# Sums of squares of single tiles: from one f32 matmul to two rounded passes, and what is reordered around them

## The chip, the core and the metric

One core of a Trainium2 chip runs the whole kernel. The metric is device time in microseconds (us); lower is better. Of the engines, TensorE (PE, its weight loads PEld), VectorE (DVE), ScalarE (ACT) and the DMA queue of SyncE (SP) work here. Each takes its instructions in the order of the program and waits on semaphores that the others raise.

## What is computed

Two encoder layers over 272 tokens (16 learned ones and 256 of the input) of width 2048. Each layer normalises its input, projects it with one matrix into the columns of four branches, and adds the projected branch outputs back:

```python
h = rms_norm(x, norm_w)
proj = jnp.einsum('bld,dn->bln', h, w_in)
(aq, ak, av, ag, bq, bk, bv, bg, cq, ckv, ckr, cg, du, dg) = jnp.split(proj, split_points, axis=-1)
ya = diff_attention(aq, ak, av, ...)      # 4 heads, rms_norm of q, k and of the head's output
yb = axial_gqa(bq, bk, bv, ...)           # 4 query heads, 2 key heads, rms_norm of q and k
yc = latent_attention(cq, ckv, ckr, ...)  # q and kv are projected up from normed latents
yd = multiscale_pool(du, ...)
y = jnp.concatenate([ya * silu(ag), yb * silu(bg), yc * silu(cg), yd * silu(dg)], axis=-1)
return x + jnp.einsum('bln,nd->bld', y, w_out)

def rms_norm(x, w):
    return x * lax.rsqrt(jnp.mean(x * x, axis=-1, keepdims=True) + EPS) * w
```

Every such norm of a query, a key or a head's output needs the sum of squares over 64 or 128 rows of a tile. It is these sums that the change is about. Layer 1 computes queries for 256 tokens only.

## The kernel before

Activations stand transposed: channels on the 128 partitions, the 272 tokens along the free axis. Weights stream from HBM into `raw` in chunks of 128 x 1024. A chunk is split into two rounded halves: ACT copies it to `w_hi` (form fp32r), DVE subtracts and writes `w_lo`. The activations are split the same way (`h_hi`/`h_lo`, `y_hi`/`y_lo`), and a product is three rounded passes (`three`, lines 725 to 727). There are four buffers of split weights (`RING`); the split of chunk s + 3 is queued in slot s, and it waits until chunk s - 1 is done.

A **slot** is the time of one chunk; there are 129 a layer. A projection of 256 columns is a **pair** of two tiles and takes four slots. The order of everything else is set by three tables, `AT_TENSOR`, `AT_SCALAR` and `AT_VECTOR`: `make_plan` gives each stage a slot, the table of an engine adds a fraction, and the engine takes its stages in the order of the sums. `MOVED` shifts single stages.

The stages that the change touches:

- `lift` (ACT) copies a finished tile out of one of two banks (`dense`); `rescale` (DVE) multiplies it with the token's norm.
- `rope_pre` (ACT) squares a tile into `sq` and, for tiles that are rotated, writes a weighted copy `qw`; `rope_stat` (PE) sums the squares over the rows with a matrix of ones in plain f32 into `norm_ps`; `rope_fin` makes the inverse root on ACT (lines 1114 and 1115, into the one buffer `rn`) and finishes the tile on DVE (five instructions, lines 1389 to 1398). Tiles aq, ak, qr and kr stand alone (11 a layer). Tiles bq, bk, qn and kn come in pairs, whose squares DVE adds first (`sq_sum`).
- `sub_pre`, `sub_stat`, `sub_fin` do the same for the output of each of the four A heads, which lies in `o_ps`. The first DVE instruction of `sub_fin` (line 1421) reads `o_ps` and signals `o_taken`. The next head's first `pv` (PE, line 924) writes that bank and waits for it. `sub_slot` puts the stage off where a slot is taken by a tile of its kind.
- `score`, `s_max`, `s_exp`, `s_scale`, `p_turn`, `p_out`, `pv` are the steps of one block of queries: PE, DVE, ACT, DVE, PE, ACT, PE.
- Slots 16 to 20 are the up-projection of branch C. Its 13 tiles go through the same two banks, so that a tile waits until `up_out` (ACT) has copied the one before the last. `up_out` copies all tiles of a chunk in one stage.
- Slots 21 to 28 do the gates of branch C (`gate`) and the norms of kr, qn, kn and qr.

Of the kernel before, what the change touches and what calls it, by code (L numbers as in the profile page):

```python
# [110 lines left out]
def score_steps(layer):  # L111
# [13 lines left out]
AT_SCALAR = dict(rope_fin=-0.166, lat_fin=0.07, mix_out=0.09, lat_pre=0.097, sub_fin=0.1, rope_pre=0.11,  # L125
                 y_split=0.66, xscale=0.283, sub_pre=0.439, x_out=0.55, p_out=0.56, gate=0.65, s_exp=0.579,
                 lift=0.6, up_out=0.705, split=0.71, x_square=0.72, y_gate=0.73, y_lat=0.72, lam_exp=0.793, v_out=1.297)
AT_VECTOR = dict(sq_sum=0.2, rope_mid=0.25, s_max=-0.418, lam_dot=-0.35, sub_fin=-0.345, rope_fin=-0.34, lat_fin=0.055, head_out=0.17,
# [4 lines left out]
MOVED = {**{("lift", l, 3, 0): -0.55 for l in range(DEPTH)},  # L133
# [4 lines left out]
def make_plan(at_engine):  # L138
# [17 lines left out]
    for l in range(DEPTH):  # L156
# [49 lines left out]
        at(s + 8, ("rope_pre", l, "kr", 0, None))  # L206
        at(s + 9, ("rope_stat", l, "kr", 0))
        at(s + 10, ("rope_fin", l, "kr", 0))

        for c in range(U_CHUNKS):  # L210
            at(s + 4 + c, ("up_out", l, c))
        posts = [("qn", 0), ("kn", 0), ("qr", 0), ("qr", 1), ("qn", 1), ("kn", 1)]
        for n, (key, i) in enumerate(posts):
            s = g0 + pair_slot(4) + 1 + n + (2 if i else 0)
            at(s, ("rope_pre", l, key, i, None))
            if key in PAIRED:
                at(s, ("sq_sum", "rope", l, key, i))
# [39 lines left out]
def build(nc, xt, w_stream, params, lam_rows, consts, out):  # L257
# [31 lines left out]
    sq = sb("sq", [128, 4, L])  # L289
    qw = sb("qw", [128, 2, L])  # L290
# [27 lines left out]
    ident, ones, halves = const("ident", 128), const("ones", 128), const("halves", 128)  # L318

# [59 lines left out]
    lam_ready, lam_exp = sem("lam_ready"), sem("lam_exp")  # L379
    tails_zero = sem("tails_zero")  # L380
# [100 lines left out]
    for stg in vector_plan:  # L481
# [7 lines left out]
        if stg[0] == "sq_sum":  # L489
# [226 lines left out]
    def _(pe):  # L716
# [102 lines left out]

        def norm_free(*stage):  # L820
# [17 lines left out]
        def rope_stat(l, key, i):  # L838
            t0 = rope_from(l, key)
            if key in PAIRED:  # L840
                pe.wait_ge(summed, sum_no[("rope", l, key, i)])
            else:
                pe.wait_ge(pre_done, pre_no[("rope_pre", l, key, i)])
            norm_free("rope_stat", l, key, i)
            sums = nc.tensor.matmul(norm_ps[:, t0:L], halves, sq[:, 2 * parity("rope_stat", l, key, i), t0:L],  # L845
                                    start=True, stop=True)
# [62 lines left out]
        def pv(l, n):  # L909
# [4 lines left out]
            if branch == "c":  # L914
                pe.wait_ge(up_taken, UP_TILES * (l + 1))
# [27 lines left out]
    def _(act):  # L943
# [98 lines left out]
        def up_out(l, c):  # L1042
            for j in range(up_tiles(c)):
                ps = wait_tile(act, l, "up", c, j)
                q0 = first_query(l)
                if c < 2:
                    i, out_ = 2 * c + j, q_st[:, 2 * c + j, q0:L]
                    free = (scores_ready, store_free(l, "c", "q", i))
                elif c == 2:
                    out_, free = c_st[:, 6 + j, q0:L], (scores_ready, store_free(l, "c", "q", j))  # L1050
                elif c == 3:
                    out_, free = k_st[:, j, :], (scores_ready, store_free(l, "c", "k", j))
                else:
                    n = K_BLOCKS[j][1]
                    out_, free = v_st[0:n, j, :], (pv_done, sums_before[store_free(l, "c", "v", 3)])
                if free[1]:
                    act.wait_ge(*free)
                src = ps[0:K_BLOCKS[j][1], :] if c == 4 else ps[:, 0:L - q0] if c < 3 else ps[:, 0:L]
                signal(nc.scalar.activation(out_, src, ACT.Copy), up_taken, UP_TILES * l + up_no(c, j))  # L1059

# [8 lines left out]
        def rope_pre(l, key, i, j):  # L1069
# [31 lines left out]
        def sub_pre(l, n):  # L1101
# [3 lines left out]
            signal(nc.scalar.activation(sq[:, 2 * parity("sub_stat", l, n), t0:L], o_ps[:, t0:L], ACT.Square), pre_done,  # L1105
# [68 lines left out]
        def s_exp(l, n):  # L1174
# [6 lines left out]
            for m in (0, 1):  # L1181
                signal(nc.scalar.activation(probs[0:nq, k % 2, m, :], s_ps[m][0:nq, 0:L], ACT.Exp,  # L1182
                                            bias=stat[0:nq, 2 + m:3 + m], scale=SCALE[b],
                                            accum_out=stat[0:nq, 4 + m:5 + m]), exp_done, 2 * k + m + 1)

        def p_out(l, n):
# [7 lines left out]
            for m in range(1 if b == "a" else 2):  # L1194
# [4 lines left out]
                if m == 0 and b != "a":  # L1199
# [5 lines left out]
                   up_out=up_out, rope_pre=rope_pre,  # L1205
# [9 lines left out]
    def _(dve):  # L1215
# [49 lines left out]
        def lam_dot(_):  # L1265
# [6 lines left out]
            signal(nc.vector.memset(stat[:, :], 0.0), lam_ready, 1)  # L1272

        def lam_out(_):
            dve.wait_ge(lam_exp, 1)
            for l in range(DEPTH):
# [5 lines left out]
                link(nc.vector.tensor_scalar(sub_w[:, c], pcol(l, "sub"), 1.0 - li, None, ALU.mult))  # L1282
# [47 lines left out]
        def sq_sum(what, l, key, i=None):  # L1330
# [14 lines left out]
            signal(nc.vector.tensor_tensor(a, a, b, ALU.add), summed, n)  # L1345

# [70 lines left out]
        def sub_fin(l, n):  # L1417
# [3 lines left out]
            signal(nc.vector.scalar_tensor_tensor(ta[:, t0:L], o_ps[:, t0:L], sub_w[:, l:l + 1], rn[:, t0:L],  # L1421
# [47 lines left out]
        def s_max(l, n):  # L1469
# [187 lines left out]
```

## Time and profile before

| | before |
|---|---|
| median of 3 runs | 913.04 us (912.84 to 913.1) |
| the profiled execution, its own time | 912.77 us |
| its span, first to last instruction | 911.0 us |
| granted TensorE clock | 1.00 (the level of 2.4 GHz) throughout |
| busy: PE / DVE / ACT | 99% / 70% / 64% of the span |

The profiled execution lies 0.27 us under the median of the runs. PE's busy time is modelled: matmuls overlap, so the time that counts is from the start of one to the start of the next. In the timeline an idle stretch stands behind an instruction in brackets, with what ended it; in the tables of stretches each engine's busy time stands with its number of instructions.

### The profile page before, as it was taken

What the parts mean: (1) busy time and instruction counts of PE and PEld (TensorE: products, weight loads), DVE (VectorE), ACT (ScalarE), POOL (GpSimd) and SP (SyncE); (2) the same over time, 40 slices, a digit from 0 to 9 for tenths busy, and PEclk for the clock granted to TensorE, in tenths of its full rate; (3) what the DMA queues carried; (4) which work ended last, traced back from release to release, by engine and by line L of the source; (5) the groups of instructions that cost most, each with busy time, mean ns of one, the idle gap of its engine ahead of it and who ended that gap; (6) DMA issues with size and microseconds to landing.
All of it is one profiled execution on the core that took longest, in us unless ns stands there. A gap on an engine that the chain in (4) does not pass through costs nothing.

```text
span 911.0 us, 18111 instructions
## 1 busy us (share of the span) xinstructions
PE 899.7 (99%) x7054; PEld 858.4 (94%) x7054; DVE 637.0 (70%) x1071; ACT 585.5 (64%) x1045; POOL 0.2 (0%) x4
## 2 busy tenths in 40 slices
PE   8999999999999999999999999999999999999998
PEld 7998998999999999999999989999999999999998
DVE  7785887768777776766665658876687667666552
ACT  7678756678666667745554588566686666675331
POOL 0000000000000000000000000000000000000000
PEclk9999999999999999999999999999999999999999
DMA  8654343343444343445455544334425344445562
GB/s 332 260 188 142 134 142 132 109 139 129 140 141 142 138 148 128 145 149 192 166 195 185 186 155 169 119 119 161 158 93 186 128 151 145 149 171 185 187 201 78
DMA packets 22997, 143.83 MB, mean 158 GB/s; under 512 B 2560, under 2 KB 4736, under 8 KB 6528
## 3 DMA queue, kind: packets, MB, share of 16 engines
q1 hardware_dynamic: 22768, 142.64, 44.0%
q8 instruction: 56, 0.92, 0.4%
q14 instruction: 29, 0.24, 0.1%
q10 hardware_dynamic: 144, 0.04, 0.0%
HBM read 140.57 MB, written 2.10 MB: 157 GB/s over the span
## 4 chain that ended last, share of the span: by engine, by line
PE 89%; ACT 7%; DVE 2%; issue 1%; DMA 1%; SPq 0%; ACTq 0%; DVEq 0%
PE dense L725 25%; PE dense L727 24%; PE dense L726 24%; PE s_ps L889 4%; PE o_ps L924 4%; ACT w_hi L1014 2%; PE norm_ps L845 2%; PE t_ps L905 2%; DVE w_lo L1319 1%; ACT qw L1087 1%; DMA x<-xt_dram 1%; PE swap_ps L860 0%; ACT sq L1084 0%; PE norm_ps L727 0%; PE swap_ps L727 0%
## 5 line engine op out<-in xcount | busy, mean ns | idle before, releaser
L725 PE MATMUL dense<-h_hi,w_hi 128*128 128x272 f32 (+2 forms) x1440 | 427.1, 297 | 1.5 <-DVE h_lo L1299 0.9
L727 PE MATMUL dense<-h_hi,w_lo 128*128 128x272 f32 (+2 forms) x1440 | 412.6, 287 | 0.0
L726 PE MATMUL dense<-h_lo,w_hi 128*128 128x272 f32 (+2 forms) x1440 | 410.6, 285 | 0.0
L1319 DVE TENSOR_TENSOR w_lo<-raw,w_hi 128x1024 fp32r<-128x1024 f32 (+1 forms) x257 | 313.3, 1219 | 88.4 <-ACT w_hi L1014 82.3
L1014 ACT ACTIVATE w_hi<-raw 128x1024 fp32r<-128x1024 f32 (+1 forms) x257 | 271.3, 1056 | 68.7 <-PE dense L727 53.9
L725 PEld LDWEIGHTS dense<-h_hi,w_hi 128*128 128x128 f32 x1440 | 271.3, 188 | 8.2 <-issue 3.8
L726 PEld LDWEIGHTS dense<-h_lo,w_hi 128*128 128x128 f32 x1440 | 271.5, 189 | 1.3
L727 PEld LDWEIGHTS dense<-h_hi,w_lo 128*128 128x128 f32 x1440 | 271.1, 188 | 0.0
L725 PE MATMUL dense<-y_hi,w_hi 128*128 128x272 f32 (+1 forms) x500 | 143.1, 286 | 2.3 <-ACT q_st L1059 1.3
L727 PE MATMUL dense<-y_hi,w_lo 128*128 128x272 f32 (+1 forms) x500 | 142.7, 285 | 0.0
L726 PE MATMUL dense<-y_lo,w_hi 128*128 128x272 f32 (+1 forms) x500 | 142.4, 285 | 0.0
L725 PEld LDWEIGHTS dense<-y_hi,w_hi 128*128 128x128 f32 x500 | 94.3, 189 | 3.5 <-issue 1.9
L727 PEld LDWEIGHTS dense<-y_hi,w_lo 128*128 128x128 f32 x500 | 94.4, 189 | 0.0
L726 PEld LDWEIGHTS dense<-y_lo,w_hi 128*128 128x128 f32 x500 | 94.0, 188 | 0.0
L1039 ACT ACTIVATE row<-dense 128x272 f32<-128x272 f32 (+2 forms) x80 | 31.4, 393 | 68.7 <-PE dense L727 67.8
L1475 DVE TENSOR_REDUCE stat<-s_ps 128x1 f32<-128x272 f32 (+1 forms) x80 | 35.1, 439 | 35.6 <-PE s_ps L889 33.6
L1327 DVE TENSOR_TENSOR row<-row,rinv 128x272 f32<-128x272 f32 (+2 forms) x80 | 34.9, 437 | 29.6 <-ACT row L1039 27.5
L1114 ACT ACTIVATE rn<-norm_ps,eps_c 128x272 f32<-128x272 f32 (+1 forms) x50 | 24.2, 484 | 35.6 <-PE norm_ps L845 24.1
L1182 ACT ACTIVATE probs<-s_ps,stat 128x272 f32<-128x272 f32 (+1 forms) x80 | 38.9, 486 | 11.5 <-DVE stat L1476 9.0
L1308 DVE TENSOR_TENSOR x<-x,dense 128x272 f32<-128x272 f32 (+1 forms) x28 | 12.0, 429 | 46.7 <-PE dense L727 46.7
L924 PE MATMUL o_ps<-p_t,v_st 128*128 128x128 f32 (+1 forms) x288 | 38.6, 279 | 1.1 <-ACT p_t L1198 1.1
L924 PEld LDWEIGHTS o_ps<-p_t,v_st 128*128 128x128 f32 x288 | 35.9, 191 | 2.7 <-ACT p_t L1198 2.2
(161 smaller groups left out, 813.4 us busy)
## 6 DMA issues: line engine op xcount, KB each, us to landing
raw<-w_stream_dram SPq DMA_DIRECT2D x128, 1024.0 KB, 4.8
out_dram<-x SPq DMA_DIRECT2D x8, 256.0 KB, 6.3
x<-xt_dram SPq DMA_DIRECT2D x3, 544.0 KB, 8.9
raw<-w_stream_dram SPq DMA_DIRECT2D x3, 512.0 KB, 7.5
con<-consts_dram SPq DMA_DIRECT2D x1, 984.0 KB, 7.4
x<-xt_dram SPq DMA_DIRECT2D x2, 272.0 KB, 4.8
raw<-w_stream_dram SPq DMA_DIRECT2D x2, 256.0 KB, 4.6
d_w<-consts_dram SPq DMA_DIRECT2D x2, 256.0 KB, 5.1
```

What stands on the lines that cost most here:

```text
L725: nc.tensor.matmul(ps, whi, xhi, start=first, stop=False)
L726: nc.tensor.matmul(ps, whi, xlo, start=False, stop=False)
L727: return nc.tensor.matmul(ps, wlo, xhi, start=False, stop=last)
L889: mm = nc.tensor.matmul(s_ps[m][0:nq, 0:L], queries[half, q:q + nq], keys[half, :], start=n_part == 0, stop=n_part == len(parts) - 1)
L924: mm = nc.tensor.matmul(o_ps[:, c:c + nq], v_st[:, b, 128 * vh:128 * vh + 128], p_t[:, m, b, 0:nq], start=b == 0, stop=b == 2)
L1014: signal(nc.scalar.activation(w_hi[:, g % RING, 0:n], raw[:, e % RAW, CHUNK * half:CHUNK * half + n], ACT.Copy), hi_ready, g + 1)
L1039: signal(nc.scalar.activation(tile_place(l, p, j), ps[:, 0:L - tile_from(l, kind, j)], ACT.Copy), lifted, scaled_no[(l, p, j)])
L1114: link(nc.scalar.activation(rn[:, t0:L], norm_ps[:, t0:L], ACT.Ln, scale=1.0 / width, bias=eps_c[:, 0:1]))
L1182: signal(nc.scalar.activation(probs[0:nq, k % 2, m, :], s_ps[m][0:nq, 0:L], ACT.Exp, bias=stat[0:nq, 2 + m:3 + m], scale=SCALE[b], accum_o ...
L1319: signal(nc.vector.tensor_tensor(w_lo[:, g % RING, 0:n], raw[:, e % RAW, CHUNK * half:CHUNK * half + n], w_hi[:, g % RING, 0:n].bitcast(F3 ...
L1327: signal(nc.vector.tensor_tensor(out_, out_, rinv[:, tile_from(l, PAIRS[p][0], j):L], ALU.mult), scaled, scaled_no[(l, p, j)])
L1475: link(nc.vector.reduce_max(stat[0:nq, m:m + 1], s_ps[m][0:nq, 0:L], AX.X))
```

## The change

- The 15 single sums of squares a layer (aq, ak, kr, qr and the A heads) are no longer one f32 matmul but two rounded passes (`two`), with the rounded squares `sq_hi` and the rest `sq_lo`. ACT writes `sq_hi` with one more copy in `rope_pre` and `sub_pre`; DVE writes `sq_lo` in a new stage `sq_low`, and PE waits for that (`summed`). The matrices of ones are copied to the rounded form once.
- Those `rope_stat`, `sub_stat`, `rope_fin` and `sub_fin` stages come one slot later.
- `rope_pre` moves from 0.11 to 0.62 of its slot, behind the lifts and the steps of the blocks of queries. `sq_sum` of the paired tiles moves from 0.2 to 0.64.
- `up_out` copies one tile a stage. In the first three chunks the second tile's copy stands behind the split of the weights. The split for chunk 18 is queued a slot earlier.
- Small buffers are merged: `lam_sum`, `neg_lam`, `sub_w`, `eps_c` and `one_c` move into other tensors.

```diff
+UP_TILES = (2, 2, 2, 4, 3)
-AT_SCALAR = dict(... rope_pre=0.11,
-                 ... up_out=0.705, split=0.71, ... y_lat=0.72, ...)
-AT_VECTOR = dict(sq_sum=0.2, ...
+AT_SCALAR = dict(... rope_pre=0.62,
+                 ... up_out=0.705, up_next=0.715, split=0.71, ... y_lat=0.74, ...)
+AT_VECTOR = dict(sq_sum=0.64, sq_low=0.64, lat_sum=0.2, ...
-MOVED = {**{("lift", l, 3, 0): -0.55 for l in range(DEPTH)},
+MOVED = {**{("lift", l, 3, 0): -0.55 for l in range(DEPTH)}, **{("split", l, 18): -0.98 for l in range(DEPTH)},
...
                     at(s, ("rope_pre", l, kind, i0 + j, j))
-                    at(s, ("rope_stat", l, kind, i0 + j))
-                    at(s + 1, ("rope_fin", l, kind, i0 + j))
+                    at(s, ("sq_low", "rope", l, kind, i0 + j))
+                    at(s + 1, ("rope_stat", l, kind, i0 + j))
+                    at(s + 2, ("rope_fin", l, kind, i0 + j))
...
         for c in range(U_CHUNKS):
-            at(s + 4 + c, ("up_out", l, c))
+            for j in range(UP_TILES[c]):
+                at(s + 4 + c, ("up_next" if c < 3 and j else "up_out", l, c, j))
...
                 at(s, ("sub_pre", l, n))
-                at(s, ("sub_stat", l, n))
-                at(s + 1, ("sub_fin", l, n))
-                at(s + 1, ("y_split", "sub_fin", l, n))
+                at(s, ("sq_low", "sub", l, n))
+                at(s + 1, ("sub_stat", l, n))
+                at(s + 2, ("sub_fin", l, n))
+                at(s + 2, ("y_split", "sub_fin", l, n))
...
+        def two(ps, table, hi, lo):
+
+            nc.tensor.matmul(ps, table, hi, start=True, stop=False)
+            return nc.tensor.matmul(ps, table, lo, start=False, stop=True)
...
-            square = nc.scalar.activation(sq[:, 2 * half, t0:L], src, ACT.Square)
-            if branch:
-                link(square)
-                square = nc.scalar.activation(qw[:, half, t0:L], src, ACT.Copy, scale=pcol(l, key))
-            signal(square, pre_done, pre_no[("rope_pre", l, key, i)])
+            link(nc.scalar.activation(sq[:, 2 * half, t0:L], src, ACT.Square))
+            link(nc.scalar.activation(qw[:, half, t0:L], src, ACT.Copy, scale=pcol(l, key)))
+            signal(nc.scalar.activation(sq_hi[:, half, t0:L], sq[:, 2 * half, t0:L], ACT.Copy),
+                   pre_done, pre_no[("rope_pre", l, key, i)])
...
+        def sq_low(what, *of):
...
+            signal(nc.vector.tensor_tensor(sq_lo[:, half, t0:L], sq[:, 2 * half, t0:L],
+                                           sq_hi[:, half, t0:L].bitcast(F32), ALU.subtract), summed,
+                   sum_no[(what, *of)])
```

What the tables do to the order is seen at three places, all in layer 0. The first is ACT in the up-projection, from the copy of its first tile on (line 1059 before, 1075 after); `dense0` and `dense1` are the two banks, `w_hi` are splits, `y_hi<-c_st` is the split of the latent ckv. Before:

```order
L1059 ACTIVATE q_st<-dense0 128x272
L1059 ACTIVATE q_st<-dense1 128x272
L1014 ACTIVATE w_hi<-raw 128x1024
L1143 ACTIVATE y_hi<-c_st 128x544
L1059 ACTIVATE q_st<-dense0 128x272
L1059 ACTIVATE q_st<-dense1 128x272
L1014 ACTIVATE w_hi<-raw 128x1024
```

and after the change:

```order
L1075 ACTIVATE q_st<-dense0 128x272
L1030 ACTIVATE w_hi<-raw 128x1024
L1075 ACTIVATE q_st<-dense1 128x272
L1160 ACTIVATE y_hi<-c_st 128x544
L1075 ACTIVATE q_st<-dense0 128x272
L1030 ACTIVATE w_hi<-raw 128x1024
L1075 ACTIVATE q_st<-dense1 128x272
```

The split now stands between the two tiles of a chunk, and the third tile's copy no longer waits behind the second split. The second place is ACT at the end of the up-projection, where the tile kr is squared (`sq<-c_st`) and weighted (`qw<-c_st`) and the last tiles (`v_st`) are copied. Before:

```order
L1014 ACTIVATE w_hi<-raw 128x1024
L1084 ACTIVATE sq<-c_st 128x272
L1087 ACTIVATE qw<-c_st,par 128x272
L1059 ACTIVATE v_st<-dense0 128x512
L1059 ACTIVATE v_st<-dense1 128x512
L1059 ACTIVATE v_st<-dense0 16x512
L1014 ACTIVATE w_hi<-raw 128x1024
```

and after:

```order
L1030 ACTIVATE w_hi<-raw 128x1024
L1075 ACTIVATE v_st<-dense0 128x512
L1075 ACTIVATE v_st<-dense1 128x512
L1075 ACTIVATE v_st<-dense0 16x512
L1030 ACTIVATE w_hi<-raw 128x1024
L1100 ACTIVATE sq<-c_st 128x272
L1101 ACTIVATE qw<-c_st,par 128x272
L1102 ACTIVATE sq_hi<-sq 128x272
```

The work on kr moved behind the last tile and the split, and is one copy longer. The third place is DVE in slots 56 to 58, around the first A head's `sub_fin` (`tab<-o_ps`, then `yt<-tab,g_st`); ahead of both pieces stands the `s_scale` of the same block (it ends in `probs<-probs,stat`). Before:

```order
L1489 SCALAR_TENSOR_TENSOR probs<-probs,stat 128x272
L1421 SCALAR_TENSOR_TENSOR tab<-o_ps,sub_w,rn 128x272
L1423 TENSOR_TENSOR yt<-tab,g_st 128x272
L1319 TENSOR_TENSOR w_lo<-raw,w_hi 128x1024
L1327 TENSOR_TENSOR row<-row,rinv 128x272
L1327 TENSOR_TENSOR row<-row,rinv 128x272
```

and after, where the lines 1417 to 1426 are a `rope_fin` and 1371 is `sq_low`:

```order
L1517 SCALAR_TENSOR_TENSOR probs<-probs,stat 128x272
L1371 TENSOR_TENSOR sq_lo<-sq,sq_hi 128x272
L1417 STREAM_SHUFFLE tab<-qw 128x272
L1418 TENSOR_TENSOR tab<-tab,con 128x272
L1419 TENSOR_TENSOR tab<-qw,con 128x272
L1420 TENSOR_TENSOR tab<-tab 128x272
L1426 TENSOR_TENSOR q_st<-tab,rn 128x272
L1336 TENSOR_TENSOR w_lo<-raw,w_hi 128x1024
L1344 TENSOR_TENSOR row<-row,rinv 128x272
L1344 TENSOR_TENSOR row<-row,rinv 128x272
L1503 TENSOR_REDUCE stat<-s_ps 128x1
L1503 TENSOR_REDUCE stat<-s_ps 128x1
```

Behind this piece come line 1504 and only then `sub_fin` (line 1449, `tab<-o_ps,par,rn`): a `rope_fin`, a split, two rescales and the next block's `s_max` now stand ahead of it.

## Rows read from the trace of the kernel before

**Rows 1.** Page: busy time of the engines; shares of the chain that ended last.
```profile
PE 899.7 (99%) x7054; PEld 858.4 (94%) x7054; DVE 637.0 (70%) x1071; ACT 585.5 (64%) x1045; POOL 0.2 (0%) x4
PE 89%; ACT 7%; DVE 2%; issue 1%; DMA 1%; SPq 0%; ACTq 0%; DVEq 0%
```
**Rows 2.** Groups by shape, TensorE: `rope_stat` on 272 tokens; count | busy us, mean ns.
```profile
L845 PE MATMUL norm_ps<-sq,con 128*128 128x272 f32 x52 | 17.2, 412 | 0.4 <-ACT qw L1087 0.4
```
**Rows 3.** Timeline, TensorE, a `rope_stat` in slot 21: start us, length us.
```profile
77.81 0.29 PE L727 MATMUL dense<-h_hi,w_lo 128*128 128x272 f32 x1
77.94 0.62 PE L845 MATMUL norm_ps<-sq,con 128*128 128x272 f32 x2
...
78.52 0.28 PE L726 MATMUL dense<-h_lo,w_hi 128*128 128x272 f32 x1
```
**Rows 4.** Timeline, TensorE, up-projections: before a wait, and behind waits.
```profile
63.03 0.29 PE L727 MATMUL dense<-y_hi,w_lo 128*128 128x272 f32 x1
63.91 0.36 PE L725 MATMUL dense<-y_hi,w_hi 128*128 128x272 f32 x1 [0.59 <-ACT q_st L1059]
...
68.47 0.39 PE L725 MATMUL dense<-y_hi,w_hi 128*128 128x272 f32 x1 [0.49 <-ACT k_st L1059]
...
73.52 0.41 PE L725 MATMUL dense<-w_hi,y_hi 128*16 128x512 f32 x1 [0.37 <-ACT v_st L1059]
...
525.66 0.36 PE L725 MATMUL dense<-y_hi,w_hi 128*128 128x256 f32 x1 [0.68 <-ACT q_st L1059]
```
**Rows 5.** Timeline, ScalarE, in the same up-projection of layer 0.
```profile
63.37 0.82 ACT L1059 ACTIVATE q_st<-dense 128x272 f32<-128x272 f32 x2
...
71.85 0.43 ACT L1084 ACTIVATE sq<-c_st 128x272 f32<-128x272 f32 x1
72.32 0.52 ACT L1087 ACTIVATE qw<-c_st,par 128x272 f32<-128x272 f32 x1
...
75.18 0.59 ACT L1059 ACTIVATE v_st<-dense 16x512 f32<-16x512 f32 x1 [1.08 <-PE dense L727]
```
**Rows 6.** Stretches: length, busy PE, PEld, DVE, ACT, POOL; clock, DMA.
```profile
75.18:90.86 15.68, 15.68 (x121) 15.20 (x120) 10.80 (x18) 14.50 (x24) 0.00 (x0) 1.00 0.38 128
212.15:214.53 2.38, 2.38 (x21) 2.38 (x21) 2.24 (x6) 2.25 (x7) 0.00 (x0) 1.00 0.78 330
218.16:221.50 3.34, 3.34 (x26) 2.81 (x26) 3.16 (x6) 2.51 (x5) 0.00 (x0) 1.00 0.29 61
```
**Rows 7.** Groups by shape, ScalarE and VectorE: a rounded copy, a difference.
```profile
L1143 ACT ACTIVATE y_hi<-c_st 128x272 fp32r<-128x272 f32 x4 | 1.7, 431 | 0.1
L1405 DVE TENSOR_TENSOR y_lo<-c_st,y_hi 128x272 fp32r<-128x272 f32 x4 | 1.8, 442 | 0.1
```
**Rows 8.** Timeline, VectorE, before chunk 28 of layer 0.
```profile
90.94 1.04 DVE L1372 SCALAR_TENSOR_TENSOR k_st<-k_st,par,rn 128x272 f32<-128x272 f32 x2 [0.70 <-ACT rn L1115]
...
96.16 2.49 DVE L1319 TENSOR_TENSOR w_lo<-raw,w_hi 128x1024 fp32r<-128x1024 f32 x2
```
**Rows 9.** Timeline, TensorE: chunk 28 of layer 0 begins.
```profile
98.08 0.29 PE L725 MATMUL dense<-h_hi,w_hi 128*128 128x272 f32 x1
```
**Rows 10.** Timeline, VectorE, layer 0: `s_max` of step 9; `sub_fin` of the first head.
```profile
210.99 0.92 DVE L1475 TENSOR_REDUCE stat<-s_ps 128x1 f32<-128x272 f32 x2 [1.12 <-PE s_ps L889]
...
217.15 0.50 DVE L1421 SCALAR_TENSOR_TENSOR tab<-o_ps,sub_w,rn 128x272 f32<-128x272 f32 x1
```
**Rows 11.** Timeline, TensorE, layer 0: the second A head's first `pv`.
```profile
223.22 0.83 PE L924 MATMUL o_ps<-p_t,v_st 128*128 128x128 f32 x6
```
**Rows 12.** Timeline, TensorE, layer 1: instructions behind waits.
```profile
549.88 0.36 PE L725 MATMUL dense<-h_hi,w_hi 128*128 128x264 f32 x1 [0.58 <-ACT row L1039]
...
619.26 0.60 PE L924 MATMUL o_ps<-p_t,v_st 128*128 128x128 f32 x3 [0.40 <-ACT p_t L1198]
...
680.45 0.72 PE L845 MATMUL norm_ps<-sq,con 128*128 128x272 f32 x2 [0.35 <-ACT qw L1087]
...
777.25 0.49 PE L924 MATMUL o_ps<-p_t,v_st 128*128 128x128 f32 x2 [0.66 <-ACT p_t L1198]
```

More of the change, by code:

```diff
@@ L839, in rope_stat @@
             t0 = rope_from(l, key)
+            pe.wait_ge(summed, sum_no[("rope", l, key, i)])
+            norm_free("rope_stat", l, key, i)
+            half = parity("rope_stat", l, key, i)
             if key in PAIRED:
-                pe.wait_ge(summed, sum_no[("rope", l, key, i)])
+                sums = nc.tensor.matmul(norm_ps[:, t0:L], halves, sq[:, 2 * half, t0:L], start=True, stop=True)
             else:
[L843 to L846, printed above, removed]
+                if (l, key) == (0, "kr"):
+                    pe.wait_ge(ones_ready, 1)
+                sums = two(norm_ps[:, t0:L], halves_r, sq_hi[:, half, t0:L], sq_lo[:, half, t0:L])
             sums.then_inc(stat_done, 1)
@@ L914, in pv @@
             if branch == "c":
-                pe.wait_ge(up_taken, UP_TILES * (l + 1))
+                pe.wait_ge(up_taken, sum(UP_TILES) * (l + 1))
             else:
@@ L928, in sub_stat @@
         def sub_stat(l, n):
-            pe.wait_ge(pre_done, pre_no[("sub_pre", l, n)])
+            pe.wait_ge(summed, sum_no[("sub", l, n)])
             norm_free("sub_stat", l, n)
             t0 = first_query(l)
-            nc.tensor.matmul(norm_ps[:, t0:L], ones, sq[:, 2 * parity("sub_stat", l, n), t0:L],
-                             start=True, stop=True).then_inc(stat_done, 1)
+            half = parity("sub_stat", l, n)
+            two(norm_ps[:, t0:L], ones_r, sq_hi[:, half, t0:L], sq_lo[:, half, t0:L]).then_inc(stat_done, 1)
         run = dict(setup=warm_up, chunk=chunk, xsum=xsum, rope_stat=rope_stat, lat_stat=lat_stat, v_turn=v_turn, mix=mix,
@@ L1040, in lift, with up_out @@
                    scaled_no[(l, p, j)])
[L1042 to L1059, printed above, removed]
+        def up_out(l, c, j):
+            ps = wait_tile(act, l, "up", c, j)
+            q0 = first_query(l)
+            if c < 2:
+                i, out_ = 2 * c + j, q_st[:, 2 * c + j, q0:L]
+                free = (scores_ready, store_free(l, "c", "q", i))
+            elif c == 2:
+                out_, free = c_st[:, 6 + j, q0:L], (scores_ready, store_free(l, "c", "q", j))
+            elif c == 3:
+                out_, free = k_st[:, j, :], (scores_ready, store_free(l, "c", "k", j))
+            else:
+                n = K_BLOCKS[j][1]
+                out_, free = v_st[0:n, j, :], (pv_done, sums_before[store_free(l, "c", "v", 3)])
+            if free[1]:
+                act.wait_ge(*free)
+            src = ps[0:K_BLOCKS[j][1], :] if c == 4 else ps[:, 0:L - q0] if c < 3 else ps[:, 0:L]
+            signal(nc.scalar.activation(out_, src, ACT.Copy), up_taken, sum(UP_TILES) * l + up_no(c, j))
         def buffers_free(*stage):
@@ L1104, in sub_pre @@
             buffers_free("sub_stat", l, n)
-            signal(nc.scalar.activation(sq[:, 2 * parity("sub_stat", l, n), t0:L], o_ps[:, t0:L], ACT.Square), pre_done,
+            half = parity("sub_stat", l, n)
+            link(nc.scalar.activation(sq[:, 2 * half, t0:L], o_ps[:, t0:L], ACT.Square))
+            signal(nc.scalar.activation(sq_hi[:, half, t0:L], sq[:, 2 * half, t0:L], ACT.Copy), pre_done,
                    pre_no[("sub_pre", l, n)])
@@ L1204, in _ @@
                    x_out=x_out, split=split,
-                   up_out=up_out, rope_pre=rope_pre,
+                   up_out=up_out, up_next=up_out, rope_pre=rope_pre,
                    lat_pre=lat_pre, sub_pre=sub_pre, xscale=xscale, rope_fin=rope_fin, lat_fin=lat_fin,
@@ L1345, in sq_sum @@
             signal(nc.vector.tensor_tensor(a, a, b, ALU.add), summed, n)
+        def sq_low(what, *of):
+            stage = ("rope_stat" if what == "rope" else "sub_stat", *of)
+            l = of[0]
+            t0 = rope_from(l, of[1]) if what == "rope" else first_query(l)
+            dve.wait_ge(pre_done, pre_no[(("rope_pre" if what == "rope" else "sub_pre"), *of)])
+            half = parity(*stage)
+            signal(nc.vector.tensor_tensor(sq_lo[:, half, t0:L], sq[:, 2 * half, t0:L],
+                                           sq_hi[:, half, t0:L].bitcast(F32), ALU.subtract), summed,
+                   sum_no[(what, *of)])
         def rope_mid(l, key, i):
```

64 lines of the change are left out of this document (34 added, 30 removed).

## Prediction

> **What bounds the kernel now.** I read the page first: TensorE is busy for 99% of the span and 89% of the chain that ended last is its own [rows 1]. So time goes down where TensorE has less to issue or waits less, and work on the other engines counts only where TensorE waits for them. The timeline of TensorE then gives the price of issuing: a rounded pass over 272 columns starts 0.13 us after the one before (77.81, 77.94), whatever its listed length [rows 3]. The places where it starts late are few and short: three in each up-projection [rows 4], some single ones in layer 1 [rows 12]. Next I looked for stretches that are full on ScalarE or VectorE though TensorE seems to lead. There are two a layer. From 75.18 to 90.86 ScalarE works 14.50 of 15.68 us [rows 6]; then VectorE, from 90.94 on, has no gap until the split of chunk 28 is ready at 97.39, and chunk 28 starts at 98.08 [rows 8, 9]. And around the first A head VectorE goes from one step's `s_max` to the next [rows 10].
>
> **The sums of squares.** A f32 sum costs 78.52 - 77.94 = 0.58 us from its start to that of the next pass, 0.13 of it the place of a pass, so 0.45 in all [rows 3]; its listed mean of two records, 412 ns, is length and not issue time [rows 2]. Two rounded passes take 2 x 0.126 = 0.25, so each sum gives 0.20 us back (0.19 where layer 1 has 256 columns). There are 30, hence 5.9 us if nobody waits. Bounds: 0 if a pair takes as long as the f32 form, 0.33 if the second pass slips beside other work. I take 0.20, from the dense passes that it resembles.
>
> The Trainium skill ("FP8 and Floating Point Precision", section "TensorE Precision Notes") says that true fp32 makes four passes through the array. The row gives 0.454 / 0.126 = 3.6 of them. By four passes a sum would give 0.25 back, and the 16 or so sums below whose gain is not lost to a wait would be worth 0.8 us more; the row decides, and no other number here uses the rule.
>
> **What is added.** 30 copies on ScalarE at 0.43 us and 30 differences on VectorE at 0.44 [rows 7], 13 us on each. Both engines are idle for a third of the span, and the sum is now taken a slot later, which leaves it 3 us for some 0.9 us of work. So they cost nothing outside the two full stretches, where they cost their whole length. The copy of the matrices of ones (one instruction, an estimate of 0.4 us), the weight scaled in place and the merged buffers lie in ScalarE's and VectorE's idle time before the up-projection; uncovered they would cost under 0.5 us once.
>
> **The up-projection.** Its three waits for `up_out` are 0.59, 0.49 and 0.37 us in layer 0; each costs more than its idle time, since the next start slips too: 63.91 - 63.03 = 0.88 against 0.13, so 0.75 for the first [rows 4]. By the same 0.15 the three cost 1.95; in layer 1 (0.68, then as before) 2.0. ScalarE copies both tiles in one go, 0.82 each, and then splits [rows 5]. After the change the first tile's bank is free before the split and the second right behind it, with no `kr` work ahead of the last copies. I expect all six gone: -1.95 and -2.0, if the chunks behind can be started earlier.
>
> **The first full stretch (slots 20 to 28).** ScalarE starts its run at 75.18 because it waited 1.08 us for TensorE's last tiles [rows 5]; after the change it starts 1.95 earlier, at 73.2. But `kr`'s square and weighted copy (0.43 + 0.52) stood before 75.18, in that idle time, and now stand behind. Two rounded copies (`kr`, `qr`) are new, 2 x 0.46 with the gap between instructions. Less about 0.45 of idle time within the stretch this makes 15.66 + 0.95 + 0.92 - 0.45 = 17.1, so the root for `kn` is there at 90.3 (was 90.84). VectorE's relay behind it takes what it took, 97.39 - 90.84 = 6.55: split 28 ready at 96.9. TensorE could be at chunk 28 at 98.08 - 1.95 - 2 x 0.20 = 95.7. So a new wait of 1.2 us stands there, and of 2.35 won only **1.1** stays. In layer 1 a wait for a lift stands there already (0.58 [rows 12]); I take **0.9**. Bounds: 0 (the relay ends no earlier) to 2.35.
>
> **The second full stretch (slots 53 to 62).** Before, `sub_fin`'s first instruction (217.15 to 217.65) frees `o_ps`, and the second head's first `pv` starts at 223.22, 5.6 us later [rows 10, 11]. After, ahead of `sub_fin` stand two differences, a `rope_fin` (2.38) and a split with rescales and `s_max` (3.34) [rows 6]. From the `s_max` at 210.99 VectorE took 217.65 - 210.99 = 6.66; after it takes 6.66 + 2 x 0.47 + 2.38 + 3.34 = 13.3. The `s_max` itself waits for TensorE [rows 10], so its start does not move against TensorE. TensorE needs 223.22 - 210.99 = 12.23 to reach that `pv`, 11.6 with three cheaper sums. The `pv` waits 13.3 - 11.6 = 1.7. What is late next is `p_turn`, `p_out` and the following `pv`, behind a VectorE that is later by those differences; I allow 0.2 in layer 0 and 0.45 in layer 1, and 2.0 for layer 1's `pv`. So layer 0 loses 1.9 against five sums (1.0): **+0.9**. Layer 1 loses 2.45 against five sums and the 0.35 wait for a square, with its restart (1.45): **+1.0**. Bounds of each: -1.0 (no wait) to +3.8 (all 4.3 us of new VectorE work plus 0.45 passed on).
>
> **The rest.** Slots 29 to 46: five sums a layer, 1.0. `rope_pre` now follows the steps of the blocks, and differences stand on VectorE, so I expect a short wait of a `pv` for `p_out`: 0.4 in layer 0, **-0.6** net. In layer 1 such a wait of 0.40 is there [rows 12] and grows to about 0.9 with its restart, **-0.3** net. Bounds of the new wait: 0 to 2. Later slots: three `sub_stat` a layer, **-0.6** and -0.57; and the wait of 0.66 at 777.25 [rows 12] goes, since the square ahead of that `p_out` moves behind it: **-1.2** in layer 1.
>
> **Sum.** Layer 0: -1.1 - 0.6 + 0.9 - 0.6 = -1.4. Layer 1: -0.9 - 0.3 + 1.0 - 1.2 = -1.4. Against the profiled 912.77 that is 909.97; the median of the runs is 0.27 above the profiled one, so 910.2. The measurement can tell 0.2%, 1.8 us, from no change: below 911.2 is faster, above 914.9 slower.
>
> **Rivals.**
> - *VectorE keeps pace (A).* Around the first A head the 13.3 us turn out 2 us shorter, since a queue of ready work runs closer together, and neither `pv` waits: -1.0 and -1.45 in place of +0.9 and +1.0, so 905.9. For it: 5.6 us of room before. Against: its pieces are all listed lengths from a stretch that is already dense. Chance 0.10.
> - *The relay to chunk 28 swallows the up-projection (B).* ScalarE's run in slots 20 to 28 lengthens by 1.1 us more than I reckon; no net gain there in either layer: 912.2, no change. For it: nothing in that chain is waited for by choice, each piece is on the path. Against: most of the lengthening is 0.43 us copies, counted. Chance 0.18.
> - *Slower (C).* VectorE has no room around the first A head: every us put ahead of `sub_fin` and of the next `s_max` in order (1.9 of differences and 2.4 of `rope_fin`, with 0.45 for `p_turn`, 4.75 a layer) comes out on TensorE. The two stretches then cost 3.75 and 3.3 rather than 0.9 and 1.0: 910.2 + 5.15 = 915.4. It decides from 3.3 us a stretch on. For it: `sub_fin` is put behind another step's `s_max`, and each step needs VectorE twice. Against: the 5.6 us. Chance 0.14.
> - *No gain per sum (D).* A rounded pair, with its reload of the ones between other passes, takes as long as the f32 form: the 16 sums that are not in a waiting stretch lose 0.2 each, 913.4. Against: 3.6 passes for the f32 form [rows 3]. Chance 0.04.
>
> **Chances and range.** The forecast has 0.54, its own range 908.6 to 911.4. Faster: 0.50 of that and A, 0.60. Same: 0.04 of it, B and D, 0.26. Slower: C, 0.14. The range leaves C out and the lower half of A: 906.5 to 913.8.
>
> **What will show it.** Right: the start of a rounded pair to the next pass at 0.25; no `up_out` in TensorE's waits in slots 16 to 20; chunk 28 of layer 0 waiting about 1 us for `w_lo`, that being ready 0.5 earlier than 97.39; the second A head's first `pv` waiting 1.5 to 2 for VectorE's `tab`; no waits at 777. Wrong: no wait at that `pv` (A), or one over 3 and late scores behind it (C); chunk 28 starting at 98 as before (B); 0.4 a pair (D). The forecast also fails if single waits for `pre_done` or `summed`, which I put at nothing, stand before the sums: 30 of them at 0.1 us would take half the gain away.

## The result: 914.56 us, no gain

| | before | after |
|---|---|---|
| median of 21 runs | 913.0 us | 914.56 us (913.7 to 915.3) |
| ratio after / before | | 1.0017 (95% interval 1.001 to 1.0023) |
| profiled execution, its own time / span | 912.77 / 911.0 us | 914.45 / 912.6 us |
| runs with a mean granted TensorE clock of 1.00 | | 10 of 21, median 914.05 us |
| runs with 0.997 or 0.998 | | 11 of 21, median 914.87 us |

The forecast was 910.2, in a range up to 913.8; the kernel became 1.6 us slower. That is inside the 0.2% that I called no change, but the interval lies above 1, so the small loss is real. Where a median below has a second one in brackets, that is the median of the runs at clock 1.00. The page after, in the rows that answer to [rows 1]: busy time, and the chain's shares.

```profile
PE 895.1 (98%) x7054; PEld 856.1 (94%) x7054; DVE 649.7 (71%) x1101; ACT 598.8 (66%) x1076; POOL 0.2 (0%) x4
PE 83%; DVE 8%; ACT 6%; issue 1%; DMA 1%; SPq 0%; ACTq 0%; DVEq 0%
```

TensorE has less work, as it should, and the chain has moved: VectorE's share went from 2% to 8%. The timeline of TensorE after shows where it waits now (start, length, idle time in brackets and what ended it):

```profile
84.21 0.70 PE L856 MATMUL norm_ps<-sq,con 128*128 128x272 f32 x2 [0.91 <-ACT rn L1132]
...
92.12 0.36 PE L829 MATMUL norm_ps<-sq_hi,sums_of 128*128 128x272 f32 x1 [0.71 <-ACT rn L1132]
92.32 0.28 PE L830 MATMUL norm_ps<-sq_lo,sums_of 128*128 128x272 f32 x1
92.44 0.28 PE L732 MATMUL dense<-h_hi,w_hi 128*128 128x272 f32 x1
...
98.58 0.39 PE L732 MATMUL dense<-h_hi,w_hi 128*128 128x272 f32 x1
...
224.17 0.91 PE L938 MATMUL o_ps<-p_t,v_st 128*128 128x128 f32 x6 [1.70 <-DVE tab L1449]
...
546.18 0.67 PE L856 MATMUL norm_ps<-sq,con 128*128 128x256 f32 x2 [1.34 <-ACT rn L1132]
...
553.79 0.36 PE L829 MATMUL norm_ps<-sq_hi,sums_of 128*128 128x256 f32 x1 [0.76 <-ACT rn L1132]
...
583.44 0.44 PE L919 MATMUL o_ps<-con,probs 128*128 128x128 f32 x2 [0.49 <-DVE yt L1459]
...
617.33 0.44 PE L919 MATMUL o_ps<-con,probs 128*128 128x128 f32 x2 [1.32 <-DVE yt L1459]
...
678.88 0.91 PE L938 MATMUL o_ps<-p_t,v_st 128*128 128x128 f32 x6 [2.23 <-DVE tab L1449]
```

The waits of the up-projections [rows 4] are gone but for about 0.1 us in each. In their place stand two waits a layer for a root (`rn`) that I had not forecast, the two at `pv` that I had, and two in layer 1 for `yt`. For the differences (`sq_lo`), whose waits the prediction put at nothing, TensorE waits twice, 0.5 us in all. ScalarE's timeline has the other half of the first pair, the last row being the root for kn:

```profile
11.64 1.06 ACT L1030 ACTIVATE w_hi<-raw 128x1024 fp32r<-128x1024 f32 x1 [1.82 <-DMA raw<-w_stream_dram]
...
74.08 0.59 ACT L1075 ACTIVATE v_st<-dense 16x512 f32<-16x512 f32 x1 [0.79 <-PE dense L734]
...
83.12 0.49 ACT L1131 ACTIVATE rn<-norm_ps,stat 128x272 f32<-128x272 f32 x1
...
88.02 0.40 ACT L1055 ACTIVATE row<-dense 128x272 f32<-128x272 f32 x1 [0.76 <-PE dense L734]
...
91.54 0.43 ACT L1132 ACTIVATE rn<-rn 128x272 f32<-128x272 f32 x1
```

And VectorE's has the two splits of which the first releases chunk 28, and around the first A head the `s_max` and the first instruction of `sub_fin`:

```profile
97.29 2.49 DVE L1336 TENSOR_TENSOR w_lo<-raw,w_hi 128x1024 fp32r<-128x1024 f32 x2
...
210.65 0.92 DVE L1503 TENSOR_REDUCE stat<-s_ps 128x1 f32<-128x272 f32 x2 [1.78 <-PE s_ps L903]
...
223.52 0.50 DVE L1449 SCALAR_TENSOR_TENSOR tab<-o_ps,par,rn 128x272 f32<-128x272 f32 x1
```

Kr's root, at 79.47 before, now begins at 83.12, right ahead of qn's sum, and at 88.02 ScalarE stands idle for a tile. ScalarE's first row is a start effect of the single execution: a chunk of weights came late and chunk 16 begins 0.54 us later than before. It isn't the change: a run below with the same code there (`e10_a_as_before`) begins chunk 16 at 58.56, just as before, and one with the start of the kernel before (`e3_up_only`) at 59.04. So the table takes the 0.54 out. It compares the two profiled executions by the starts of their chunks:

| slots | forecast | measured |
|---|---|---|
| layer 0, 16 to 28 | -1.1 | +0.05 |
| 29 to 52 | -0.6 | -0.46 |
| 53 to 62 | +0.9 | +0.59 |
| later | -0.6 | +0.12 |
| layer 1, 16 to 28 | -0.9 | +0.23 |
| 29 to 52 | -0.3 | +0.33 |
| 53 to 62 | +1.0 | +1.20 |
| later | -1.2 | -0.95 |
| sum | -2.8 | +1.1 |

### The profile page after: what moved, and what is told of

Its sections match the earlier page's. It is cut to its first block, busy times and chain, and to the rows that moved or that the text cites. A ratio compares the mean times of both kernels' runs of the same rounds, so it can differ in the third digit from the quotient of the medians.

```text
span 912.6 us, 18203 instructions
## 1 busy us (share of the span) xinstructions
PE 895.1 (98%) x7054; PEld 856.1 (94%) x7054; DVE 649.7 (71%) x1101; ACT 598.8 (66%) x1076; POOL 0.2 (0%) x4
## 4 chain that ended last, share of the span: by engine, by line
PE 83%; DVE 8%; ACT 6%; issue 1%; DMA 1%; SPq 0%; ACTq 0%; DVEq 0%
PE dense L732 23%; PE dense L734 23%; PE dense L733 23%; PE s_ps L903 4%; PE o_ps L938 3%; ACT w_hi L1030 2%; DVE w_lo L1336 2%; PE t_ps L919 1%; DVE stat L1503 1%; DMA raw<-w_stream_dram 1%; PE norm_ps L856 1%; ACT qw L1101 1%; PE swap_ps L874 1%; DVE tab L1417 1%; DVE tab L1420 0%
## 5 line engine op out<-in xcount | busy, mean ns | idle before, releaser
L1131 ACT ACTIVATE rn<-norm_ps,stat 128x272 f32<-128x272 f32 (+1 forms) x50 | 24.2, 484 | 26.7 <-PE norm_ps L856 7.7
```

The source lines that it names most:

```text
L1131: link(nc.scalar.activation(rn[:, t0:L], norm_ps[:, t0:L], ACT.Ln, scale=1.0 / width, bias=eps_c[:, 0:1]))
```

## Experiments

Nine kernels were measured, beside runs of the kernel before (912.96 to 912.98 in each set). Times are medians.

**Slots 16 to 28: kr's place or ScalarE's load?** My first theory was that kr's later place costs. The first run puts kr's stages back, with its copies:

```diff
-        at(s + 9, ("rope_pre", l, "kr", 0, None))
-        at(s + 9, ("sq_low", "rope", l, "kr", 0))
-        at(s + 10, ("rope_stat", l, "kr", 0))
-        at(s + 11, ("rope_fin", l, "kr", 0))
+        at(s + 7.49, ("rope_pre", l, "kr", 0, None))
+        at(s + 8, ("sq_low", "rope", l, "kr", 0))
+        at(s + 9, ("rope_stat", l, "kr", 0))
+        at(s + 10, ("rope_fin", l, "kr", 0))
```

> The changed kernel with the stages of kr alone at their old slots and its rope_pre ahead of the last v_st copies. Theory (kr's place): kr's sum one slot later stands right ahead of qn's, both in the one bank norm_ps; ScalarE reaches kr's root late, TensorE waits 0.91 and 0.71 us (layer 0), 1.34 and 0.76 (layer 1) for it and for the next root, and ScalarE then waits for TensorE. With kr back these waits shrink to under half and the time falls by 2.2 us, 1.1 a layer, to about 912.4. Rival (load): ScalarE is short by its added copies wherever they stand; the wait moves to chunk 28 and the time falls by less than 0.7 us.

Measured: 913.64 (913.58), at clock 1.00 0.47 less than the changed kernel, which is the rival's size. The second leaves kr where the change put it and takes away the load, the copies and differences of kr and qr:

```diff
+            if key in ("kr", "qr"):
+                signal(weighted, pre_done, pre_no[("rope_pre", l, key, i)])
+                return
...
-            if key in PAIRED:
+            if key in PAIRED or key in ("kr", "qr"):
                 sums = nc.tensor.matmul(norm_ps[:, t0:L], halves, sq[:, 2 * half, t0:L], start=True, stop=True)
```

> The changed kernel with the sums of kr and qr in f32 again, without their copies and differences, and kr where the change puts it. Putting kr back with its copies brought 0.0 us in layer 0 and 0.5 in layer 1. Theory (ScalarE's load in slots 20 to 28): two copies of 0.46 less let kn's root come 0.9 earlier, TensorE's waits for roots shrink by as much, and after the dearer f32 sums 0.6 us a layer stay: 913.3. Rival (kr's place, next to qn in the one bank): the waits at 83 and 91 us stay as they are, and the time rises by the f32 sums, to about 915.

Measured: 913.18 (912.37), at clock 1.00 1.7 less, so the theory and not the rival. The third has both undone:

> The changed kernel with kr and qr wholly as before: f32 sums, no copies, no differences, kr at its old slots; the rest of the change stays. Load and place together: slots 16 to 28 then run as in the run with the up-projection alone, 0.87 us a layer under the kernel before, so 0.9 and 1.1 us less than the changed kernel: 912.5. If neither load nor place is the cause, the time stays within 0.3 us of 914.5.

Measured: 912.86 (912.27), as the theory had it. The fourth is the kernel before with the up-projection's part alone (`up_out` by tiles, `up_next`, the split for chunk 18):

> The kernel before with one part of the change alone: up_out copies one tile a stage, the second behind the split, and the split for chunk 18 is queued earlier. f32 sums, kr and all else as before. Theory (kr's place): the three waits of each up-projection go (1.95 and 2.0 us); kr's two passes stay in ScalarE's idle time, so most of it is kept: 3.0 us less than before, about 910.0. Rival (the relay to chunk 28 swallows it whatever kr does): within 0.5 us of before, with a new wait of 1 us or more between slots 21 and 28 in each layer.

Measured: 911.46, ratio to before 0.9985 (0.9976 to 0.9994): half of the theory's gain. The lengths of slots 16 to 28, layer 0 and layer 1, in the kernel before, in the changed one, with kr early, with f32 sums in branch C and kr late, with kr and qr as before, and with the up-projection alone (the view of stretches, columns as in [rows 6]):

```profile
58.56:103.13 44.57, 43.12 (x310) 39.75 (x311) 29.80 (x46) 37.31 (x63) 0.00 (x0) 1.00 0.49 175
520.56:564.10 43.54, 41.42 (x312) 38.09 (x311) 29.47 (x46) 36.85 (x63) 0.00 (x0) 1.00 0.48 172
```
```profile
59.10:103.72 44.62, 42.94 (x310) 39.91 (x311) 30.57 (x48) 37.35 (x65) 0.00 (x0) 1.00 0.47 168
521.40:565.17 43.77, 41.48 (x312) 38.31 (x311) 30.21 (x48) 36.85 (x65) 0.00 (x0) 1.00 0.46 166
```
```profile
58.70:103.29 44.59, 42.90 (x310) 39.80 (x311) 30.59 (x48) 37.35 (x65) 0.00 (x0) 1.00 0.47 165
520.97:564.23 43.26, 41.49 (x312) 38.20 (x311) 30.24 (x48) 36.89 (x65) 0.00 (x0) 1.00 0.46 167
```
```profile
58.53:102.29 43.76, 43.21 (x311) 40.10 (x311) 29.29 (x45) 36.10 (x62) 0.00 (x0) 1.00 0.49 174
520.18:563.12 42.94, 41.77 (x313) 38.60 (x311) 28.95 (x45) 35.65 (x62) 0.00 (x0) 1.00 0.47 172
```
```profile
58.69:102.59 43.90, 43.15 (x310) 39.96 (x311) 29.29 (x45) 36.10 (x62) 0.00 (x0) 1.00 0.48 173
520.47:563.01 42.54, 41.65 (x312) 38.44 (x311) 28.95 (x45) 35.65 (x62) 0.00 (x0) 1.00 0.48 172
```
```profile
59.04:102.73 43.69, 43.24 (x311) 39.84 (x311) 29.48 (x46) 37.10 (x63) 0.00 (x0) 1.00 0.48 176
520.15:562.84 42.69, 41.55 (x312) 38.24 (x311) 28.51 (x45) 36.04 (x62) 0.00 (x0) 1.00 0.48 177
```

The place theory falls in layer 0, where kr early saves 0.03 us. In layer 1 its place is worth some of the loss: 0.51 us with the copies, and 0.40 without them (42.94 less 42.54). In layer 0 the waits only move, as the timelines of TensorE show. With kr early, one is back in the up-projection, and qr's stays:

```profile
73.13 0.41 PE L732 MATMUL dense<-w_hi,y_hi 128*16 128x512 f32 x1 [0.92 <-ACT v_st L1075]
...
91.68 0.36 PE L829 MATMUL norm_ps<-sq_hi,sums_of 128*128 128x272 f32 x1 [0.71 <-ACT rn L1132]
```

Without the load, kr late, both waits for roots shrink from 0.91 and 0.71 to a quarter of a microsecond (in layer 1 from 1.34 and 0.76 to 0.72 and 0.30):

```profile
83.20 0.70 PE L859 MATMUL norm_ps<-sq,con 128*128 128x272 f32 x2 [0.24 <-ACT rn L1139]
...
90.65 0.70 PE L859 MATMUL norm_ps<-sq,con 128*128 128x272 f32 x2 [0.25 <-ACT rn L1139]
```

The stretch is 0.86 and 0.83 us shorter than the changed kernel's, about the two copies (2 x 0.46). Copies and differences were taken away together, so that ScalarE alone is at fault is read from the rows, which name its `rn`, and not separated. The run with the up-projection alone gains 0.88 and 0.85 us by chunk 29 and had as much at chunk 21: chunk 28 swallows nothing when nothing is added. It isn't the 1.95 and 2.0 of the forecast because kr's two passes still stand ahead of the last copies there, and a wait of 0.45 us for `v_st` stays.

One more thing holds ScalarE up in the changed kernel: `rope_pre` of qr stands behind the two lifts. Two of the kernels on record show what that is worth. The run with kr and qr as before leaves it there, and ScalarE idles ahead of the second lift; the last run of this section has it ahead of the lifts as before, and both lifts go in one go:

```profile
87.32 0.40 ACT L1058 ACTIVATE row<-dense 128x272 f32<-128x272 f32 x1 [0.87 <-PE dense L734]
```
```profile
87.19 0.83 ACT L1093 ACTIVATE row<-dense 128x272 f32<-128x272 f32 x2
```

Counted from chunk 16, kn's root is there after 32.12 us in the first and 31.28 in the second, 0.84 earlier. (The two differ in `sq_sum`'s place too.) Of that, 0.3 us reaches TensorE in layer 0.

**The first A head: order or amount of work on VectorE?** `sub_fin` put ahead of the rescales and `s_max`:

```diff
-         ("rescale", 0, 20, 1): 1.01, ("split", 1, 101): 0.95}
+         ("rescale", 0, 20, 1): 1.01, ("split", 1, 101): 0.95, ("sub_fin", 0, 8): -0.12, ("sub_fin", 1, 5): -0.12}
```

> The changed kernel with sub_fin of the first A head of each layer ahead of the two rescales and s_max on VectorE, nothing else moved. Theory (order on VectorE): the pv waits of 1.70 and 2.23 us go, and the s_max that is now 0.95 us later reaches TensorE nowhere: 3.5 to 4.2 us less, about 910.6. Rival (amount of work on VectorE): the wait only moves to p_turn or the following pv, less than 1 us gained.

Measured: 916.01 (916.22), at clock 1.00 worse by 2.2. The wait at `pv` goes, and others come: 1.83 and 0.79 us in layer 1, and these three in layer 0:

```profile
227.80 0.39 PE L829 MATMUL norm_ps<-sq_hi,sums_of 128*128 128x272 f32 x1 [1.14 <-DVE sq_lo L1371]
...
232.46 0.36 PE L829 MATMUL norm_ps<-sq_hi,sums_of 128*128 128x272 f32 x1 [0.79 <-ACT rn L1132]
...
237.14 0.32 PE L919 MATMUL t_ps<-con,probs 16*128 16x16 f32 x3 [1.19 <-DVE probs L1517]
```

By the order of the rows, what is pulled ahead of `s_max` delays the next block's chain, and so the following difference and `p_turn`: VectorE has no room there. Not even the rival allowed for a loss. The counter-test takes the work away: the sums of the stretch are f32 again, in their old slots.

```diff
+def in_f32(stage):
+
+    what, l, key = stage[:3]
+    if what == "sub_stat":
+        return key == (8, 5)[l]
+    return key in ("aq", "ak") and stage[3] >= 2
```

> The changed kernel with the stretch around the first A head as before in both layers: the sums of the second aq and ak pairs and of the first A head in f32, without copies and differences, in their old slots with the old fraction of rope_pre; all else as the change has it. Theory (VectorE has no room for a rope_fin and differences more ahead of sub_fin, and after the 2.23 us wait in layer 1 TensorE's granted clock falls in half of the executions): both pv waits go, 0.8 us in layer 0 and 1.2 in layer 1, about 912.0 at full clock, and no execution has a mean granted clock under 0.999. Rival (the waits come from the first stretch's delay or from elsewhere): the pv waits stay over 1 us, or clocks of 0.998 stay in half of the executions.

Measured: 911.27, all 11 runs at 0.999 or 1.00, and no wait at either `pv`:

```profile
222.82 0.83 PE L967 MATMUL o_ps<-p_t,v_st 128*128 128x128 f32 x6
...
675.90 0.83 PE L967 MATMUL o_ps<-p_t,v_st 128*128 128x128 f32 x6
```

That is 2.8 us under the changed kernel at full clock, more than the 2.0 expected: slots 53 to 62 are 1.11 us shorter than in the changed kernel in layer 0 and 1.70 in layer 1. The run undoes the differences, the later slots and the copies of these sums together, so it shows that they make the waits, and not which of them.

**The price of a sum.** f32 sums again, with copies, differences and order left as changed:

```diff
-                sums = two(norm_ps[:, t0:L], halves_r, sq_hi[:, half, t0:L], sq_lo[:, half, t0:L])
+                sums = nc.tensor.matmul(norm_ps[:, t0:L], halves, sq[:, 2 * half, t0:L], start=True, stop=True)
...
-            two(norm_ps[:, t0:L], ones_r, sq_hi[:, half, t0:L], sq_lo[:, half, t0:L]).then_inc(stat_done, 1)
+            nc.tensor.matmul(norm_ps[:, t0:L], ones, sq[:, 2 * half, t0:L], start=True, stop=True).then_inc(stat_done, 1)
```

> The changed kernel with f32 sums again (one f32 matmul of sq in place of the two rounded passes); the copies, differences, waits and the order all stay. Theory (a sum gives 0.20 us back where TensorE leads): 16 to 20 of the 30 sums count, 3.2 to 4.0 us more, about 918. Rival (a rounded pair is no cheaper): within 0.5 us of the changed kernel. All 30 counted would be 5.9 us more.

Measured: 915.78, 1.73 more than the changed kernel at full clock. At 0.20 a sum that is 9 of the 30; the others stood where TensorE waits for something else anyway, and these waits shrink instead (at `pv` from 1.70 to 1.08 us and from 2.23 to 1.69). Neither side had put it so low.

**Is the later slot to blame?** Rounded sums of aq, ak and the A heads in their old slots, on top of branch C as before:

```diff
-                    at(s + 1, ("rope_stat", l, kind, i0 + j))
-                    at(s + 2, ("rope_fin", l, kind, i0 + j))
+                    at(s, ("rope_stat", l, kind, i0 + j))
+                    at(s + 1, ("rope_fin", l, kind, i0 + j))
...
-                at(s + 1, ("sub_stat", l, n))
-                at(s + 2, ("sub_fin", l, n))
+                at(s, ("sub_stat", l, n))
+                at(s + 1, ("sub_fin", l, n))
```

> As the run with kr and qr as before, and besides the rounded sums of aq, ak and the A heads in the slots that the f32 sums had, rope_pre and sq_sum at their old fractions, these sums at the end of their slot (0.87). Theory (the slot, not the two passes, is what costs): the waits at pv around the first A head and those for yt in layer 1 go, as rope_fin and sub_fin are where they were; 24 sums give 0.20 back each where nothing waits: 907 to 909. Rival (the differences alone load VectorE too much, or the sums now wait for them): at most 1.5 us less than with the slots of the change, about 911.

Measured: 925.18, 12 us more than the run it builds on; both theories fall. All four runs have a lowered clock, but the one at 0.998 takes 923.99, so most of the loss isn't the clock. One of its sums on TensorE, and what VectorE did ahead of it:

```profile
167.88 0.40 PE L831 MATMUL norm_ps<-sq_hi,sums_of 128*128 128x272 f32 x1 [2.40 <-DVE sq_lo L1380]
```
```profile
163.73 0.46 DVE L1426 STREAM_SHUFFLE tab<-qw 128x272 f32<-128x272 f32 x1
...
166.13 1.23 DVE L1345 TENSOR_TENSOR w_lo<-raw,w_hi 128x1024 fp32r<-128x1024 f32 x1
167.39 0.44 DVE L1380 TENSOR_TENSOR sq_lo<-sq,sq_hi 128x272 fp32r<-128x272 f32 x1
```

The difference stands behind a `rope_fin` and a split in VectorE's queue, and the sum now hangs on it. So a slot of slack is needed once VectorE is in the path.

**What pays, together.** The up-projection's part, and rounded sums only for the three later A heads of each layer and aq, ak 0 and 1 of layer 0:

```diff
+    if what == "sub_stat":
+        return key == (8, 5)[l]
+    return key in ("kr", "qr") or key in ("aq", "ak") and (l == 1 or stage[3] >= 2)
```

> The parts that paid, together: the up-projection's copies one tile a stage; kr, qr, the second aq and ak pairs, the first A head and all of layer 1's aq and ak as before (f32, old slots); rounded pairs a slot later only for the later A heads of both layers and for aq and ak 0 and 1 of layer 0; the square of layer 1's second bq pair at the late place. Theory (a rounded sum pays 0.20 us where ScalarE and VectorE have room): 911.46 less 1.2 for six A heads, 0.4 to 0.8 for four tiles, 0.6 for the wait at 777 us: 909.0 to 909.4. Rival (each moved sum finds a new wait): 911 or more.

Measured: 908.78 us, the lowest run 908.49 and the highest 908.94, ratio to before 0.9954 (0.9941 to 0.9966): faster than both kernels, and a little lower than the theory. TensorE has 89% of the chain again, as before:

```profile
PE 89%; ACT 6%; DVE 4%; issue 1%; DMA 0%; SPq 0%; ACTq 0%; DVEq 0%
```

## Why the prediction was wrong

- **The sums.** The pair's price was right: 92.44 less 92.12 is 0.32 behind a wait, and 0.25 where TensorE runs on. What failed is the count. I let the 16 sums outside the waiting stretches come through in full; the run with f32 sums shows the worth of 9 of 30. In it the chunks behind a single sum move by 0.18 to 0.22 us each, so the f32 form does cost 3.6 of the rounded passes. I had set that against the four passes that the Trainium skill states ("FP8 and Floating Point Precision", section "TensorE Precision Notes"), but the trace agrees with four. In the last section passes of 272 columns start 0.227 us apart at 1.2 GHz, which is one column a clock; at 2.4 GHz that would be 0.113 us, and four of them 0.453 (an estimate), where the row has 0.454. What takes longer than its columns at 2.4 GHz is the rounded pass, with 0.126.
- **The up-projection: right in kind, 0.3 and 0.6 us too large.** Chunk 21 begins 1.63 us earlier against chunk 16 than before (forecast 1.95), in layer 1 1.44 (2.0).
- **The first full stretch: the step that failed.** I had kn's root at 90.3 and so 1.1 us kept; it came at 91.97, or 91.43 without the late start. Of the 1.1, 0.34 is a later begin of ScalarE's run (74.08 less 0.54, not 73.2), which is what the up-projection gave less. The other 0.76 is the idle time at 88.02: `rope_pre` of qr, moved behind the lifts, no longer fills the wait for the second lift (the two runs compared above bear this out). I had reckoned the run as never short of input. The two copies themselves cost their whole length, as I had it; the run without them gets 0.86 back. The 6.55 of VectorE's relay held to the hundredth (91.97 to 98.52), but the wait did not appear at chunk 28, where I looked for it: TensorE had already lost it at 84.21 and 92.12, at the bank `norm_ps`. That is rival B, which I gave 0.18; by itself it would have given 912.2. In layer 1 the stretch lost 0.23 where I had 0.9 won, and kr's place has a part in it.
- **The second full stretch: right.** VectorE took 13.37 us from `s_max` to the end of `sub_fin`'s first instruction (210.65 to 224.02; forecast 13.3), the `pv` waits are 1.70 and 2.23 (1.7 and 2.0). What the second of these waits costs besides stands in the last section.
- **The rest.** In layer 1 I had a `pv` wait for `p_out`, 0.9; the waits are 0.49 and 1.32, for VectorE's `yt`. Ahead of the second a second `rope_fin` now stands; the first is 0.30 in the runs without the copies of kr and qr, so part of it is a tail of the first stretch. In layer 0 a sum of 0.25 crosses the table's border at slot 63 (so 53 to 62 look better and the later slots worse), and the sum of the second bq pair costs 0.2 more since `sq_sum` moved too. That the waits for `yt` and of bq come from the moves is read from the order and the trace; the run of what pays together, which leaves layer 1's aq and ak and layer 0's `sq_sum` where they were, has neither.

Forecast -2.8, measured +1.0 at full clock: of the 3.8, 2.3 is the first stretch, 0.6 layer 1's `yt`, 0.7 layer 0's later slots. The last 0.5, to the median, is the clock.

## What to carry to other kernels

Work moved to engines with a third of idle time is free only where TensorE doesn't wait for them: take each full stretch by itself, and look there at every handover (a single bank, a lift that waits), not only at the end of the stretch. Shortening one engine's instruction by putting two others into its path needs slack in their queues first: with a slot of it the whole change cost 1.6 us against the kernel before, without it 12. A change of many alike edits should be cut by place: a third of the rounded sums, with the part on the up-projection, gained 4.2 us.

## What was not expected of the hardware

The run with kr and qr as before was profiled in an execution of mean clock 0.998. Stretches of it around the second layer's long wait (columns as above; the clock stands behind the busy times), and TensorE's instructions there:

```profile
674.00:676.50 2.50, 0.42 (x4) 0.20 (x2) 2.33 (x6) 0.78 (x4) 0.00 (x0) 1.00 0.54 161
...
677.57:679.50 1.93, 1.93 (x10) 1.93 (x10) 1.79 (x5) 1.80 (x5) 0.00 (x0) 0.50 0.27 115
679.50:682.47 2.97, 2.97 (x24) 2.95 (x22) 2.52 (x5) 2.84 (x5) 0.00 (x0) 0.84 0.00 0
682.47:686.41 3.94, 3.94 (x36) 3.94 (x33) 3.69 (x10) 3.37 (x7) 0.00 (x0) 1.00 0.75 270
```
```profile
676.66 1.26 PE L941 MATMUL o_ps<-p_t,v_st 128*128 128x128 f32 x6 [2.23 <-DVE tab L1456]
...
678.17 0.43 PE L734 MATMUL dense<-h_hi,w_lo 128*128 128x272 f32 x1
678.39 0.43 PE L732 MATMUL dense<-h_hi,w_hi 128*128 128x272 f32 x1
...
680.21 0.41 PE L734 MATMUL dense<-h_hi,w_lo 128*128 128x272 f32 x1
```

Behind 2.23 us of idle time TensorE is granted the level of 1.2 GHz for some microseconds; its passes start 0.227 us apart (nine from 678.17 to 680.21), not 0.126. The same wait in the changed kernel's profiled execution left the clock at 1.00, so it happens in some executions only. 11 of 21 of the changed kernel have a lowered mean clock, and they are 0.8 us slower. None of the 16 runs of the two kernels without that wait (`e10_a_as_before`, `e8_best`) was under 0.999, nor any of the six with f32 sums, where the wait is 1.69 us. Yet with the sums in their old slots the profiled execution has the clock at 0.50 behind three waits, of 2.40, 1.70 and 2.21 us, so the length of one wait doesn't settle it. With `sub_fin` ahead of `s_max`, where waits follow close on one another, three runs of 0.997 or 0.998 were no slower than the other three; perhaps a lower clock costs only where TensorE would else have run on, which these few runs don't show. In the changed kernel the wait of 2.23 us costs about a third more than its idle time, in every other run.
